# Two fused blocks on one core: mix and down finished by token tile, and branch products from halves

## The reference

```python
for l in range(2):
    h = rmsnorm(x, norm_mix_pre[l])
    qa, ka, va, pu, qc, kc, vc, gl = split(h @ w_in[l])        # 1024 -> 5888
    ya = attention(qa, ka, va); yb = pool_mixer(pu); yc = neighbourhood(qc, kc, vc)
    z = [ya, yb, yc] each @ w_branch[l]                        # 3 x (512 -> 1024)
    merged = sum(sigmoid(gl + b_gate) * z)
    x = x + rmsnorm(merged @ w_out[l], norm_mix_post[l])       # "mix"
    h = rmsnorm(x, norm_ffn_pre[l])
    up = conv3(h @ w_up[l])                                    # 1024 -> 5632
    x = x + rmsnorm((gelu(gate) * val) @ w_down[l], norm_ffn_post[l])   # "down"
```

## Time and profile before

| | |
|---|---|
| median of 3 runs (lowest, highest) | 2198.4 us (2195.64, 2199.47) |
| profiled execution | 2199.45 us, its span 2197.5 us |
| TensorE busy | 2017.9 us, 92% of the span |
| VectorE, ScalarE, GpSimd busy | 36%, 32%, 12% |
| granted TensorE clock, mean | 0.957 |
| first stage, until the first gather for the experts | 0 to 260.2 us |
| experts | 260.2 to 1267.8 us |
| first layer, with the norms ahead of it | 1267.8 to 1726.5 us |
| second layer | 1726.5 to 2186.9 us, then 10.6 us to the end |

### The profile page before, as it was taken

How to read it: one execution, slowest core, us unless ns; L and a number is a source line. 1 busy time by engine, 2 the same in 40 slices (tenths; PEclk the granted TensorE clock), 3 DMA queues, 4 the chain that set the end, 5 groups by cost and what they waited for, 6 DMA issues and landing times.

```text
span 2197.5 us, 30287 instructions
## 1 busy us (share of the span) xinstructions
PE 2017.9 (92%) x11629; PEld 1311.4 (60%) x11630; DVE 800.1 (36%) x1351; ACT 704.7 (32%) x1092; POOL 260.6 (12%) x243
## 2 busy tenths in 40 slices
PE   5998699999999999999999979997999799997998
PEld 2785333333333333333333368986998699987996
DVE  2443411211111111111211166516675475246663
ACT  2434211112111221122222145523554355415543
POOL 3040000000000000000100002000242020000340
PEclk7889699999999999999999989998999899998999
DMA  9786599999896999799999855434555354453553
GB/s 356 154 285 268 232 389 418 417 416 417 325 416 284 417 416 418 324 418 416 418 418 417 362 178 178 147 118 153 170 177 191 122 192 135 135 185 122 184 182 115
DMA packets 203793, 608.93 MB, mean 277 GB/s; under 512 B 10946, under 2 KB 115542, under 8 KB 167312
## 3 DMA queue, kind: packets, MB, share of 16 engines
q1 hardware_dynamic: 197600, 585.40, 69.8%
q0 software_dynamic: 5776, 21.35, 3.4%
q10 hardware_dynamic: 328, 0.95, 0.1%
HBM read 604.51 MB, written 9.24 MB: 279 GB/s over the span
## 4 chain that ended last, share of the span: by engine, by line
PE 70%; DMA 10%; SPq 5%; issue 5%; DVE 5%; ACT 3%; DVEq 0%; ACTq 0%
PE bank L738 33%; PE bank L995 15%; PE bank L1024 9%; DMA ring<-in_w_gate_up 7%; PE bank L1088 3%; PE bank L955 2%; SPq L619 2%; SPq L622 2%; DMA ring<-in_w_in 2%; PE bank L968 1%; PE bank L988 1%; DMA ring<-in_w_ada 1%; ACT probs L1579 1%; DVE split L1416 1%; PE bank L788 1%
## 5 line engine op out<-in xcount | busy, mean ns | idle before, releaser
L995 PE MATMUL bank<-ring,qkv 128*64 128x512 f32 x2240 | 496.5, 596 | 13.4 <-DMA ring<-in_w_gate_up 13.3
L738 PE MATMUL bank<-hT_hi,split 128*128 128x256 f32 x2432 | 443.8, 285 | 5.4 <-DVE hT_lo L1424 4.0
L738 PEld LDWEIGHTS bank<-hT_hi,split 128*128 128x128 f32 x2432 | 383.4, 194 | 8.2 <-issue 6.9
L1416 DVE TENSOR_TENSOR split<-ring,split 128x2048 fp32r<-128x2048 f32 x120 | 283.8, 2367 | 265.1 <-ACT split L1737 264.9
L1737 ACT ACTIVATE split<-ring 128x2048 fp32r<-128x2048 f32 x120 | 229.6, 1913 | 415.9 <-PE bank L738 333.7
L995 PEld LDWEIGHTS bank<-ring,qkv 128*64 128x64 f32 x2240 | 155.2, 137 | 337.7 <-issue 294.4
L738 PE MATMUL bank<-hT_lo,split 128*128 128x256 f32 x1216 | 346.3, 285 | 0.0
L1024 PE MATMUL bank<-ring,qkv 128*64 128x512 f32 x1120 | 255.8, 598 | 25.7 <-ACT qkv L1698 23.5
L738 PEld LDWEIGHTS bank<-hT_lo,split 128*128 128x128 f32 x1216 | 235.8, 194 | 0.0
L1394 DVE SCALAR_TENSOR_TENSOR out_halves<-bank,probs,out_halves 64x512 fp32r<-64x512 f32 x70 | 52.5, 750 | 395.6 <-ACT out_halves L1720 395.1
L1384 DVE TENSOR_SCALAR qkv<-bank 128x512 f32<-128x512 f32 x35 | 24.2, 692 | 423.0 <-PE bank L995 423.0
(11 more groups left out here) (281 smaller groups left out, 2306.3 us busy)
## 6 DMA issues: line engine op xcount, KB each, us to landing
ring<-in_w_gate_up SPq DMA_DIRECT2D x256, 1024.0 KB, 17.0
ring<-in_w_down SPq DMA_DIRECT2D x150, 1024.0 KB, 15.8
ring<-in_w_in SPq DMA_DIRECT2D x58, 1024.0 KB, 5.4
ring<-in_w_up SPq DMA_DIRECT2D x44, 1024.0 KB, 5.1
ring<-in_w_ada SPq DMA_DIRECT2D x24, 1024.0 KB, 10.1
ring<-in_w_out SPq DMA_DIRECT2D x12, 1024.0 KB, 6.1
ring<-in_w_branch SPq DMA_DIRECT2D x12, 1024.0 KB, 5.1
neighbours<-rpb_copies POOLq DMA_DIRECT2D x32, 128.0 KB, 9.5
```

Of the source, the lines that this page charges most:

```text
L738: last = pe.matmul(out, a[a_half], b[b_half], start=start and i == 0, stop=stop and i == 2)
L995: last = pe.matmul(hidden[q][CAP * j:CAP * j + CAP, :], xgT[:, k % 4, k // 4, :], unit_at(k)[:, c:c + 512], start=False, stop=(k == KC - 1))
L1416: dve.tensor_tensor(low, unit_at(u % RING_L), high.bitcast(F32), ALU.subtract).then_inc(low_done, 1)
```

## The change

It has these parts.

- **Last units by token tile** (`tiled_rows_product`): of the last two units of `mix` and `down` both are first multiplied for token tile 0, then both for tile 1, so that tile 0's norms can start before.
- **Norms by tile, folded into the transposes** (`first_tile`, `second_tile`, `turn_tile`, `token_halves`): `x` is no longer scaled into `htok`. TensorE multiplies each piece of `x` by a diagonal matrix of the tile's scales, a full-precision product instead of a transpose. The first three units after a norm are multiplied tile by tile. For `h` the weights move, 256 columns at a time, as before; for `g` (`across=True`) the tokens move, and one tile is 128 columns, so each piece of weights is loaded once for each tile.
- **Five pairs with low halves in place**: five slots (`SLOT_OF`), the low half written over the unit itself. Slots are loaded again when TensorE is through with them. The fifth lies in the memory of the attention, and is in use for unit 2 and from `FIRST_UP` on. The first two units of a layer are loaded and halved before it begins.
- **Branch products of halves**: the `w_branch` units are halved too, and so are the attentions' and the pool's outputs (`outs_high`, `out_low`).
- **Banks**: `plan_layer` starts at bank 4, and `down` at bank 0 (`p.at`).
- **First block**: the fox bias for odd heads uses other rows of the array, and the wait is gone. The routing takes fewer VectorE operations, and the gates' come after the positions'. The fill of `y_halves` is earlier.
- `take_low(9)` and `take_low(13)` stand between the two tiles of `normalise`, and the same with `take_high` in `exps`; GpSimd loads the norm gains later.

Its core:

```diff
+_A, _B, _C, _D, _E = range(SLOTS_L)
+SLOT_OF = [_A, _B, _E, _C, _D] + 7 * [_A, _B, _C, _D] + 3 * [_E, _A, _B, _C, _D] + 3 * [_E, _C, _D, _A, _B] + [_E, _C, _D]
...
+    def token_halves(prefix, names):
+        p.tile(f"{prefix}0")
+        p.tile(f"{prefix}1")
+        p.bank(names[0])
+        p.bank(names[1])
+        p.tile(f"{prefix}2")
+        p.tile(f"{prefix}3")
+        p.bank(names[2])
+        for n in names:
+            p.unit(n)
+    def rows(name, units):
+        for j in range(4):
+            p.bank(f"{name}{j}")
+        for u in range(units - 2):
+            p.unit(*[f"{name}{j}" for j in range(4)])
+        p.tiles += 1
+        for j in range(2):
+            p.jobs[f"{name}{j}"][2] = p.tiles
+        for u in range(2):
+            p.unit(*[f"{name}{j}" for j in (2, 3)])
...
+    p.at = 4
+    token_halves("h", IN2[0:3])
+    project(IN2[3:EARLY])
     for g in range(4):
         p.tile(f"diff{g}")
     for g in range(4):
@@ -249,20 +282,13 @@
         p.bank(f"branch{u}0")
         p.bank(f"branch{u}1")
         p.unit(f"branch{u}0", f"branch{u}1")
-    for j in range(4):
-        p.bank(f"mix{j}")
-    for u in range(4):
-        p.unit(*[f"mix{j}" for j in range(4)])
-    for j in range(4):
-        p.tile(f"g{j}")
-    for c in range(UPAIRS):
-        for n in ("val", "gate"):
-            p.bank(f"{n}{c}")
-            p.unit(f"{n}{c}")
-    for j in range(4):
-        p.bank(f"down{j}")
-    for u in range(FT // 2):
-        p.unit(*[f"down{j}" for j in range(4)])
+    rows("mix", OUT_UNITS)
+    names = [f"{n}{c}" for c in range(UPAIRS) for n in ("val", "gate")]
+    token_halves("g", names[0:3])
+    project(names[3:])
+    p.at = 0
+    rows("down", FT // 2)
+    assert p.units == N_UNITS
...
+        raw_l = [ring[:, s * UNIT:(s + 1) * UNIT] for s in range(4)] + [qkv[:, 2048:4096]]
+        low_l = [ring_r[:, s * UNIT:(s + 1) * UNIT] for s in range(4)] + [qkv_r[:, 2048:4096]]
+        high_l = [ring_r[:, (4 + s) * UNIT:(5 + s) * UNIT] for s in range(3)] + [last_high_t[:, :], qkv_r[:, 4096:6144]]
...
+            with sp.Fori(0, LAYERS) as l:
+                for u, source in list(enumerate(layer_sources(bass.ds(l, 1))))[FIRST_UNITS:]:
+                    sp.wait_ge(*released_unit(u, l))
+                    if u == FIRST_UP:
+                        sp.wait_ge(branch_ready, l * 2 + 2)
+                    load_unit(u, source)
...
+            def turn_tile(names, tt):
+                pe.wait_ge(h_ready, seen(h_ready))
+                for j, n in enumerate(names):
+                    b = take(n)
+                    for kk in range(4):
+                        c = (4 * j + kk) * P
+                        last = pe.matmul(b[:, kk * P:kk * P + P], x[:, tt, c:c + P], diag[:, tt, :], start=True, stop=True)
+                    tile(last)
+            def tile_product(name, w_halves, tt, turned_names, across):
+                b, turned_names = banks[JL[name][0]], turned_names[2 * tt:2 * tt + 2]
+                for i in range(2 if across else 1):
+                    for k in range(KC):
+                        if i == 0 and k % 4 == 0:
+                            read(turned_names[k // 4])
+                        hs = [a[:, k, tt * P:tt * P + P] for a in hT_halves()]
+                        if across:
+                            ws = [a[:, k, i * P:i * P + P] for a in w_halves]
+                            last = split_product(b[:, i * T + tt * P:i * T + tt * P + P], ws, hs, k == 0, k == KC - 1)
+                        else:
+                            ws = [a[:, k, :] for a in w_halves]
+                            last = split_product(b[:, tt * 256:tt * 256 + 256], hs, ws, k == 0, k == KC - 1)
+                return last
+            def token_halves(prefix, names, across):
+                turned_names = [f"{prefix}{j}" for j in range(4)]
+                turn_tile(turned_names[0:2], 0)
+                halves_ = []
+                for i, n in enumerate(names):
+                    if i == 2:
+                        turn_tile(turned_names[2:4], 1)
+                    take(n)
+                    halves_.append(next_halves(KC))
+                    tile_product(n, halves_[i], 0, turned_names, across)
+                for i, n in enumerate(names):
+                    used(tile_product(n, halves_[i], 1, turned_names, across))
+            def tiled_rows_product(name, rows, chunks, await_rows):
+                bs, units = [take(f"{name}{j}") for j in range(4)], chunks // 2
+                def part(u, w_halves, js):
+                    for c in range(2):
+                        f = 2 * u + c
+                        for j in js:
+                            tokens, half = slice(j // 2 * P, j // 2 * P + P), slice(j % 2 * 512, j % 2 * 512 + 512)
+                            last = split_product(bs[j][:, :], [a[:, tokens] for a in rows(f)],
+                                                 [a[:, c, half] for a in w_halves], f == 0, f == chunks - 1)
+                    return last
+                for u in range(units - 2):
+                    await_rows(u)
+                    used(part(u, next_halves(2), range(4)))
+                last_two = []
+                for u in range(units - 2, units):
+                    await_rows(u)
+                    last_two.append((u, next_halves(2)))
+                    last = part(*last_two[-1], (0, 1))
+                tile(last)
+                for u, w_halves in last_two:
+                    used(part(u, w_halves, (2, 3)))
...
                         if extra is not None:
-                            if o:
-
-                                last.then_inc(odd_scores, 1)
-                                pe.wait_ge(odd_scores, tt * PAIRS + h // 2 + 1)
-                            last = extra(b, tt, h)
...
+                token_halves("h", IN2[0:3], False)
                 for u in range(6):
                     bs = [take(f"branch{u}{i}") for i in range(2)]
-                    wv = unit_at(next_unit()).rearrange("p (k n) -> p k n", k=4)
+                    w_halves = next_halves(4)
                     for i in range(2):
                         for c in range(2):
                             n0 = (2 * i + c) * P
                             for k in range(4):
-                                last = pe.matmul(bs[i][:, c * T:c * T + T], wv[:, k, n0:n0 + P],
-                                                 mixT[:, 4 * (u // 2) + k, :], start=(k == 0), stop=(k == 3))
+                                f = 4 * (u // 2) + k
+                                last = split_product(bs[i][:, c * T:c * T + T], [a[:, k, n0:n0 + P] for a in w_halves],
+                                                     [branch_hi[:, f, :], branch_lo(f)], k == 0, k == 3)
                     used(last)
-                split_rows_product("mix", lambda f: (hT_hi[:, f, :], hT_lo[:, f, :]), KC, merged_in)
-                for tt in range(TT):
-                    pe.wait_ge(h_ready, seen(h_ready))
-                turn_h([f"g{j}" for j in range(4)], htok)
-                read(*[f"g{j}" for j in range(4)])
-                for c in range(UPAIRS):
-                    split_project_T(f"val{c}")
-                    split_project_T(f"gate{c}")
-                split_rows_product("down", lambda f: (gated_hi[:, f, :], gated_lo(f)), FT, gated_in)
+                tiled_rows_product("mix", lambda f: (hT_hi[:, f, :], hT_lo[:, f, :]), KC, merged_in)
+                up = [f"{n}{c}" for c in range(UPAIRS) for n in ("val", "gate")]
+                token_halves("g", up[0:3], True)
+                for n in up[3:]:
+                    split_project_T(n)
+                tiled_rows_product("down", lambda f: (gated_hi[:, f, :], gated_lo(f)), FT, gated_in)
...
+            def stepped(tt, signal):
+                dve.wait_ge(roots, seen(roots))
+                own(dve.reciprocal(rstd[:, tt:tt + 1], root[:, tt:tt + 1]))
+                dve.scalar_tensor_tensor(out=x[:, tt, :], in0=normed_t[:, tt, :], scalar=rstd[:, tt:tt + 1],
+                                         in1=x[:, tt, :], op0=ALU.mult, op1=ALU.add).then_inc(signal, 1)
+            def scaled_ident(tt):
+                dve.wait_ge(roots, seen(roots))
+                own(dve.reciprocal(x_rstd[:, tt:tt + 1], x_root[:, tt:tt + 1]))
+                dve.tensor_scalar(diag[:, tt, :], ident, x_rstd[:, tt:tt + 1], None, ALU.mult).then_inc(h_ready, 1)
+            def first_tile(bank_of, gate, done, signal, between=lambda: None):
+                for j in (0, 1):
+                    summed(j, bank_of, gate, done)
+                both_halves(0)
+                stepped(0, signal)
+                between()
+                scaled_ident(0)
+                for j in (2, 3):
+                    summed(j, bank_of, gate, done)
+                both_halves(1)
+            def tile_low(name, column, j, tt):
+                dve.wait_ge(hT_high, seen(hT_high))
+                for kk in range(4):
```

(50 more changed lines are left out.)

494 lines of the change are left out of this document (270 added, 224 removed).

## The result

The kernel after takes 2210.3 us (2209.6 to 2210.8 in five runs), the kernel before 2198.4 us. The ratio is 1.0055, with a 95% interval of 1.004 to 1.007. So the change makes the kernel 12 us slower, where 2179 was forecast. The span of the profiled execution grows from 2197.5 to 2209.0 us, by 11.5, where the sum had -20.0.

What follows compares the result with a forecast made beforehand. TensorE, busy 92% of the span, was taken as the bound: only its own work and holes count. Terms from -12.5 (norm between layers) to +14.4 (norms after mix) summed to -20.0, so 2179 us; range 2152 to 2198.

Steps and rivals of the forecast that it cites:

- the sum: All terms of the change added against the profiled execution's 2199.45 us: -20.0 us, so 2179 us.
- The width of a narrow product: Products of 128 columns, set by their weight loads: 0.113 us each, lower end 0.066, upper end 0.217.
- + 0.5 for the clock: In each norm after mix and between the layers: 0.5 us for the clock after idle time, where before it was 2.2.
- The prediction's own sign of being wrong: Prediction wrong if narrow products cost something else, or holes inside the norms are longer than 4 us in all.
- 0.066 and 0.081 us: Rival, chance 0.15, loads hide behind moving columns: narrow product 0.066 us, 27 us less, 2152; by the skill's 0.081, 18 less.
- The dear one: Rival, chance 0.12: a narrow product of halves runs as full-precision, 0.217 us, 60 us more, 2239; decides from 0.148 us.
- TensorE was fed: Rival, chance 0.13: the change doesn't feed TensorE; stalls of 3 us in four attentions, +12, 2192, up to 2200.
- the tilewise narrow form: Norms after mix: 288 products of 128 columns, 32.5 us instead of 17.35; 42.2 against 35.0, +7.2 each, +14.4.
- Banks: Start of down: 3.0 us wait for the last gate unit's reader, less a 0.97 us wait; 2 x 2.0 = +4.0.
- The norm between the layers: From down's end to the third unit's end: 25.5 us instead of 38.1, -12.5.
- Branches, attention, end, experts' norm: Branch products -10.6, attention's hole of 2.84 us removed -5.7, end -1.2, norm after the experts -0.5 (between -3 and +2).
- First stage: Up to the first gather, -7.9: fox attention -4.8, limited by the last `w_in` unit, and routing -3.1.

Runs made afterwards that it cites:

- the probe: The kernel after plus, behind its last product, streams of products of several widths into a free bank; narrow ones took 0.212 us each at clock 0.50; no kernel time given.

## Why the prediction was wrong

- **The width of a narrow product**: 0.113 us was right, at full clock. The step that failed is the clock term of the norms after mix, "+ 0.5 for the clock": it measured 10.5 us each, 20 us more than the two terms. (The holes there came to 4.5 and 3.3 us, where 5.5 were forecast, and give a part of it back.) I had taken it from what the clock costs before wide products (2.2 us) and cut it down for smaller holes. Behind holes of 2.6, 1.0 and 0.9 us the clock is lost, and of the 96 narrow products ahead of the second tile's turning at full precision, 84 in the first layer and all in the second run at 0.213. The prediction's own sign of being wrong, narrow products that cost something else, was the one that came.
- **The rivals** on narrow products asked only whether they are cheaper or dearer than 0.113 us as such. 0.066 and 0.081 us fell. The dear one's deciding point, 0.148 us, is close to what came, since 288 products, of which 84 to 96 take 0.213, make 0.142 to 0.146 on average. That is chance: it came by another mechanism, which I had not put up. TensorE was fed, too: of its holes in the layers, all those over 0.3 us end with VectorE or ScalarE, none with a DMA. (That the loads of both kinds have the same length is so, 190 and 194 ns, but the earlier trace rows shows only one of them.)
- **Even with the clock held**, the tilewise narrow form lost, as forecast: 150.8 us against some 142 at full width, both filled. By the sum, 288 products of 0.113 us cost 15.2 us more than 144 of 0.1205, and the order by tile wins some 6 us of start.
- **Banks**: the direction was right, the term mis-sized: 2.0 a layer was forecast, 8.0 measured. I had followed only the last unit's reader, 3.0 us, as if it could start when the unit ends. VectorE and ScalarE run a unit behind at that point, and the bank comes free 6.6 us after. The rest, 2.4 us, is the clock that this hole costs down.
- **The norm between the layers**: -7.7 instead of -12.5. The loop's jump stood between two steps of the chain, and I had left it out, though the engines did that jump in the kernel before as well. There it stands between VectorE's step on `x` and ScalarE's square of `x`:

```profile
1733.27 1.91 ACT L1737 ACTIVATE split<-ring 128x2048 fp32r<-128x2048 f32 x1 [3.78 <-issue]
```

With the loops written out this row of the table is -13.2, so the rest of the chain's arithmetic held.
- **Branches, attention, end, experts' norm**: right in sign and within 1.6 us a layer. The window of the branches is 35.9 us (36 forecast), with 1.05 us for a low half at its end (1.5 forecast). The attentions gave 1.6 us a layer more, though 0.82 us of the hole of 2.84 stayed: that hole had cost clock too, 13.3 us for the next 96 products, which take 11.8 now.
- **First stage**: -6.0 instead of -7.9. Fox attention fell to about 7 us, and two units of `w_in` are late next (5.36 and 4.89 us above), where I had one in view. The six `w_in` units issued from 60 to 150 us took 32.7 us to land (median), 5.4 in the whole program, and the write of `distances` among them 46.6. That this write delays them is argued from its place, and wasn't tried.

## What to carry to other kernels

Work by tile shortens a norm's hole, but look at what is multiplied behind the hole: here products of 128 columns, each with a load of its own, started at half clock there and stayed at it. Make the products behind a hole wide ones, or fill the hole with products nobody reads, all of it, and read the granted clock behind it. When results get other banks, find the reader of the bank that is asked for first and ask how far behind it runs and for which engine it waits, not only how long it takes.

## What the runs showed of the hardware

- A stream of products of halves with 128 moving columns, each with a load of 128, that follows 4.0 us of idle time fell to a granted clock of 0.50 in its first microsecond and stayed there for the rest of its 68 us, with TensorE busy all the time; the same stream started at 1.00 stayed at 1.00 for its 36 us. Full-precision products of 128 columns, started at 0.50, were at 1.00 after 4 us. (One execution of the probe.)
- After a stretch at 1.00, the clock dropped behind twelve narrow products with 0.57 and 0.87 us of idle time around them, in both layers, and stayed up when six products of 512 columns were put there. Around products of 256 columns, holes of 1.50 and 0.73 us left it at 1.00.
- At a loop's jump ScalarE was idle for 2.6 us and VectorE for 4.9, the last 1.9 of them with ScalarE's result there; 0.57 and 0.93 us with the loops written out. Writing two turns out cost nothing that these traces show.
- 42 products that nobody reads made the kernel after 22 us faster (21 us in the two stretches after mix); 88 made the one with wide products 8.5 us faster (8.0 us there).
